# A decoder step on one core: the index-key projection moved to the two-bank group, the indexer's products spread over three query heads, the last turned chunk copied first, the samples' final sums joined

## The reference

```
q, k, v, qi, ki, wi = jnp.split(h @ w_in, ATTN_SPLITS, axis=-1)
q = rms_norm(q.reshape(B, T, N_HEADS, HEAD_DIM), g_q)
ki = rms_norm(ki, g_kidx)
...
logits = jnp.einsum('bthd,bsd->bths', qi, ki).astype(jnp.float32) * IDX_DIM ** -0.5
w = wi.astype(jnp.float32) * IDX_HEADS ** -0.5
return jnp.einsum('bth,bths->bts', w, jax.nn.relu(logits))
...
for e in range(N_EXPERTS):
    out = out + combine[:, e:e + 1].astype(t.dtype) * swiglu(t, w_gate[e], w_up[e], w_down[e])
```

## Time and profile before

| | |
|---|---|
| median of 3 runs | 1547.24 us (1545.6 to 1547.84) |
| profiled execution | 1545.37 us, span 1543.2 us |
| PE busy | 1512.4 us, 98% of the span |
| DVE busy | 1211.9 us, 79% |
| ACT busy | 979.4 us, 63% |
| POOL busy | 166.2 us, 11% |
| mean granted clock of PE | 0.994 |

### The profile page before, as it was taken

One profiled execution on the slowest core, in us unless ns is written; L12 is line 12 of the kernel. 1 busy time (PEld: TensorE's weight loads), 2 busy tenths in 40 slices (PEclk: granted clock), 3 DMA queues, 4 the chain that ended last, 5 costly groups with the idle time before them and its releaser, 6 DMA issues.

```text
span 1543.2 us, 21704 instructions
## 1 busy us (share of the span) xinstructions
PE 1512.4 (98%) x8246; PEld 1284.9 (83%) x8246; DVE 1211.9 (79%) x1127; ACT 979.4 (63%) x928; POOL 166.2 (11%) x160
## 2 busy tenths in 40 slices
PE   7899989999999999999999999999999999999998
PEld 5787768999997987888888888888888888888886
DVE  5479774666454958889889889889888888889887
ACT  3343663444344567777777777777777777777774
POOL 2455000000000014801000000000000000100000
PEclk9899999999999999999999999999999999999999
DMA  6346773343655437999999999999999999999990
GB/s 216 117 184 257 277 267 116 127 146 123 234 199 183 168 110 255 380 382 382 393 395 382 393 395 382 394 395 392 384 395 383 381 395 372 378 395 369 375 346 31
DMA packets 199014, 457.30 MB, mean 296 GB/s; under 512 B 12104, under 2 KB 15210, under 8 KB 198954
## 3 DMA queue, kind: packets, MB, share of 16 engines
q1 hardware_dynamic: 190754, 439.27, 76.9%
q0 software_dynamic: 4416, 13.15, 3.0%
q10 hardware_dynamic: 3784, 4.06, 0.8%
HBM read 444.43 MB, written 12.03 MB: 296 GB/s over the span
## 4 chain that ended last, share of the span: by engine, by line
PE 84%; DVE 2%; ACT 1%; issue 0%; DVEq 0%; ACTq 0%
PE bank L1922 18%; PE bank L2377 13%; PE bank L2379 13%; PE bank L2378 13%; PE bank L2391 7%; PE bank L2393 6%; PE bank L2392 6%; PE bank L1909 2%; PE bank L2401 2%; PE bank L2190 1%; PE bank L1917 0%; PE bank L2284 0%; PE bank L2194 0%; DVE ring_r L1348 0%; PE bank L2358 0%
## 5 line engine op out<-in xcount | busy, mean ns | idle before, releaser
L1742 DVE TENSOR_TENSOR wql<-ring,wqh 128x2048 fp32r<-128x2048 f32 x336 | 768.8, 2291 | 108.4 <-ACT wqh L933 107.9
L933 ACT ACTIVATE wqh<-ring 128x2048 fp32r<-128x2048 f32 x336 | 644.9, 1920 | 231.0 <-PE bank L2379 147.8
L2377 PE MATMUL bank<-wqh,xgh 128*128 128x512 f32 x896 | 355.3, 396 | 0.4 <-issue 0.4
L2379 PE MATMUL bank<-wqh,xgl 128*128 128x512 f32 x896 | 349.6, 390 | 0.0
L2378 PE MATMUL bank<-wql,xgh 128*128 128x512 f32 x896 | 349.1, 390 | 0.0
L2379 PEld LDWEIGHTS bank<-wqh,xgl 128*128 128x128 f32 x896 | 168.3, 188 | 36.1
L2377 PEld LDWEIGHTS bank<-wqh,xgh 128*128 128x128 f32 x896 | 168.2, 188 | 34.7 <-issue 0.8
L2378 PEld LDWEIGHTS bank<-wql,xgh 128*128 128x128 f32 x896 | 168.4, 188 | 32.9
L933 ACT ACTIVATE wd<-ring 128x1024 fp32r<-128x1024 f32 x90 | 94.8, 1058 | 129.9 <-PE bank L1922 129.8
L2391 PE MATMUL bank<-wqh,heTh 128*128 128x512 f32 x440 | 171.4, 389 | 0.0
L2393 PE MATMUL bank<-wqh,heTl 128*128 128x512 f32 x440 | 171.2, 389 | 0.0
(11 more groups left out here) (414 smaller groups left out, 2013.7 us busy)
## 6 DMA issues: line engine op xcount, KB each, us to landing
ring<-in_moe_w_gate SPq DMA_DIRECT2D x56, 2048.0 KB, 15.5
ring<-in_moe_w_up SPq DMA_DIRECT2D x56, 2048.0 KB, 15.8
ring<-in_moe_w_down SPq DMA_DIRECT2D x56, 2048.0 KB, 14.9
ring<-in_attn_w_in SPq DMA_DIRECT2D x7, 2048.0 KB, 10.4
ring<-in_ffn_w_gate SPq DMA_DIRECT2D x5, 2048.0 KB, 8.3
ring<-in_ffn_w_up SPq DMA_DIRECT2D x5, 2048.0 KB, 8.0
ring<-in_cache_k SPq DMA_DIRECT2D x16, 512.0 KB, 13.3
ring<-in_cache_v SPq DMA_DIRECT2D x16, 512.0 KB, 5.2
```

Source lines behind the costliest of these rows:

```text
L933: return nc.scalar.activation(dst, src, ACT.Copy)
L1742: return v.tensor_tensor(dst, src, head.bitcast(F32), ALU.subtract)
L2377: mm(bank, xgh[:, k, :], w_h[:, part], start=(k == 0), stop=False)
L2379: last = mm(bank, xgl[:, k, :], w_h[:, part], start=False, stop=(k == KD - 1))
```

## The change

It has four parts.

1. `ki` moves from group A to group B. Its products stay in their place. In group A the result six places ahead of `("qk", 0)` is now `wi`. ACT makes all four first weight quarters ahead of the square `kisq`; before it made two ahead of it and one behind.
2. `kio` and `("iss", 0)` move from behind head 0 to behind head 1, `("iss", 1)` to behind head 2, `isel` to behind head 3, ahead of `("is", 0)`.
3. In the last item ACT and DVE take the last turned chunk ahead of the last weight half instead of behind it.
4. At the end the two results of the samples share one bank: the first half of the columns on partitions 0 to 31, the second on 32 to 63. The matrix `pickT` gets columns of zeros on both sides of the samples' (they are there from the memset), so that each pair of products adds zeros to the other's rows. One sum of 64 rows takes the place of two of 32, and comes last. `xtok` is loaded in the same layout, the weights of the samples are copied once to partitions 32 to 63, and the last result is stored by ACT and SP, half each.

```
-    A.add("ki", "dve")
+    B.add("ki", "dve")
...
-        if n == 0:
+        if n == 1:
             A.add("kio", "act")
-            for g in range(2):
-                A.add(("iss", g), "act")
+            A.add(("iss", 0), "act")
         elif n == 2:
+            A.add(("iss", 1), "act")
+        elif n == 3:
             A.add("isel", "dve")
...
+        sp.wait_ge(sc_ok, 5)
+        sp.dma_start(o_y[1][:, 0:CH], xtok[0:NS, 2, 0:CH]).then_inc(end_stored, 16)
+        sp.wait_ge(end_stored, 16)
...
-        heads_before(2)
-        act.wait_ge(*A.full("ki"))
-        nc.scalar.activation(kisq[:], A.ap("ki")[:, 0:T], ACT.Square).then_inc(kisq_ok, 1)
-        heads_before(3)
+        heads_before(WRING)
+        act.wait_ge(*B.full("ki"))
+        nc.scalar.activation(kisq[:], B.ap("ki")[:, 0:T], ACT.Square).then_inc(kisq_ok, 1)
...
             for p in range(3, halves if last else halves + 3):
+                if last and p == halves - 1:
+                    take_heT(i, NCH - 1, heTh2)
                 head(i, HPRO + p)
...
-                    copy(pickT[:, 0:T], banks[7][:, 0:T]).then_inc(pickT_ok, 1)
+                    copy(pickT[:, 0:NP], banks[7][:, 0:NP])
+                    copy(pickT[:, NP + NS:NP + 2 * NS], banks[7][:, NP:T]).then_inc(pickT_ok, 1)
...
-            if n == 2:
+            if n == 3:
                 take_sample_scores()
...
-            m, half = k % 3, k // 3
+            m, half, r = (k % 2, k // 2, P) if k < 4 else (2, 0, 2 * NS)
             dve.wait_ge(sc_full, k + 1)
...
+                if last and p == halves - 1:
+                    heT_tails(i, NCH - 1, heTl2, heTh2)
                 tail(i, HPRO + p)
...
+        link(v.tensor_copy(comb[NS:2 * NS, 2, 1:ITEMS + 1], comb[0:NS, 2, 1:ITEMS + 1]))
         dve_body(last_item, LAST)
-        dve.wait_ge(xtok_in, 16 * 3)
-        for k in range(6):
+        dve.wait_ge(xtok_in, 16 * 4)
+        for k in range(5):
             add_back(last_item + 1, k, banks[END_BANK[k]])
...
-        project("ki", kw, 0, None, hE)
+        B.room(pe, "ki")
+        for c in range(KD):
+            last = mm(B.ap("ki")[:, 0:T], kw[:, c, 0:P], hE[:, c, :], start=(c == 0), stop=(c == KD - 1))
+        last.then_inc(b_full, 1)
...
+        def scatter_samples(half, bank):
+
+            part, left = slice(CH * half, CH * half + CH), pickT[:, NP + NS * (1 - half):NP + NS * (1 - half) + 2 * NS]
+            mm(bank[0:2 * NS, :], left, ysbh[:, part], start=(half == 0), stop=False)
+            return mm(bank[0:2 * NS, :], left, ysbl[:, part], start=False, stop=(half == 1))
```

More of the change, by code:

```diff
@@ L917, in _ @@
         pool.sem_inc(scatters, 1)
-        for m in range(3):
-            pool.dma_start(xtok[0:ROWS[m], m, :], z_rows[P * m + P:P * m + P + ROWS[m], :]).then_inc(xtok_in, 16)
+        for m in range(2):
+            pool.dma_start(xtok[:, m, :], z_rows[P * m + P:P * m + 2 * P, :]).then_inc(xtok_in, 16)
+        for half in range(2):
+            pool.dma_start(xtok[NS * half:NS * half + NS, 2, 0:CH], z_rows[3 * P:3 * P + NS, CH * half:CH * half + CH])\
+                .then_inc(xtok_in, 16)
     @block.scalar
@@ L1016, in take_indexer @@
                 copy(kitok[0:NS, 2, :], kio[0:NS, 2, 0:ID]).then_inc(a_act, 1)
[L1017 to L1020, removed]
+            if n in (1, 2):
+                g = n - 1
+                act.wait_ge(*A.full(("iss", g)))
+                nc.scalar.activation(rls[:, g, :], A.ap(("iss", g))[:, 0:WS], ACT.Relu, scale=ID ** -0.5)\
+                  .then_inc(a_act, 1)
             elif n in SCORES:
@@ L1323, in _ @@
         act_body(last_item, LAST)
-        for k in range(6):
-            m, part = k % 3, slice(CH * (k // 3), CH * (k // 3) + CH)
+        for k in range(4):
+            m, part = k % 2, slice(CH * (k // 2), CH * (k // 2) + CH)
             act.wait_ge(sc_ok, k + 1)
-            store(rows_of(o_y, m)[:, part], xtok[0:ROWS[m], m, part])
+            store(rows_of(o_y, m)[:, part], xtok[:, m, part])
+        act.wait_ge(sc_ok, 5)
+        store(o_y[1][:, CH:D], xtok[NS:2 * NS, 2, 0:CH])
         act.wait_ge(stored, 16 * N_STORED)
@@ L2022, in indexer @@
         def indexer(n):
-            if n == 0:
+            if n == 1:
                 A.room(pe, "kio")
-                pe.wait_ge(*A.freed("ki"))
+                pe.wait_ge(*B.freed("ki"))
                 for m in range(3):
@@ L2030, in indexer @@
                 pe.wait_ge(*A.freed(("qi", 3)))
[L2031 to L2043 removed]
+            if n in (1, 2):
+                g = n - 1
+                A.room(pe, ("iss", g))
+                for j in range(4):
+                    b = 4 * g + j
+                    rows = A.ap(("iss", g))[NS * j:NS * j + NS, :]
+                    q = qix[:, b, :, :].rearrange("p h t -> p (h t)")
+                    pe.wait_ge(*A.freed(("kipt", b // 2)))
+                    mm(rows[:, 0:PAST], q, kipT[:, 2 * b:2 * b + 2, :].rearrange("p a s -> p (a s)"),
+                       start=True, stop=True)
+                    last = mm(rows[:, PAST:WS], q, kiT[:, NP + TS * b:NP + TS * b + TS], start=True, stop=True)
+                last.then_inc(a_full, 1)
+            if n == 3:
                 A.room(pe, "isel")
@@ L2462, in _ @@
         pe.wait_ge(pickT_ok, 1)
-        for k in range(6):
-            pe.wait_ge(y_ok, k // 3 + 1)
-            scatter(k, banks[END_BANK[k]])
+        for half in range(2):
+            pe.wait_ge(y_ok, half + 1)
+            for m in range(2):
+                scatter(2 * half + m, banks[END_BANK[2 * half + m]])
+            last = scatter_samples(half, banks[END_BANK[4]])
+        last.then_inc(sc_full, 1)
     return ctx
-END_BANK = [0, 1, 2, 3, 6, 7]
+END_BANK = [0, 1, 2, 3, 6]
 INS = ["x_prompt", "x_sample", "cache_k", "cache_v", "cache_kidx", "page_table", "norm_mix", "norm_ffn",
```

44 lines of the change are left out of this document (15 added, 29 removed).

## The result

The changed kernel takes 1536.63 us (median of 6 runs, 1535.95 to 1537.23), the kernel before 1546.38 (6 runs, 1544.7 to 1547.84). The ratio is 0.9934, 95% interval 0.9923 to 0.9945: 9.75 us faster by the medians. The profiled execution took 1536.29 us against 1545.37, 9.08 less; 1536.3 was worked out for it ahead of the run.

A forecast was written before the change was run, and what follows sets the result against it. TensorE, busy 98% of the span, was taken as the bound. Terms 6.6 + 1.9 + 0.6 = 9.1 us off the shown median 1547.24 gave 1538.1 (1536.3 for the profiled execution), range 1536 to 1541.5.

The forecast's parts named there:

- A: Whole kernel: the forecast that all gains arrive, 9.1 us less, median 1538.1 us; chance 0.66.
- Start, 4.45 + 1.95 + 0.2 = 6.6: Ahead of and in the first query head: idle gap 4.45, lower clock 1.95; selection's bank wait 0.2; 6.6 us gained.
- D: Rival: the start's 6.6 us come to nothing, through DVE's full stretch or an unmoved load; gain 2.5, time 1544.7; chance 0.11.
- left behind head 0, they would be wanted at 52 and wait for 53.04: Indexer at the start: transposes of kiT kept behind head 0 would wait from 52 until kiT is written at 53.04.
- the spread of the indexer: Indexer's products over three heads: the selection's wait for head 0's bank goes, 0.2 us gained.
- Last turned chunk, 1.9: Last item's end: copying the turned chunk first removes PE's wait for xgl, 1.83 to 2.0, taken as 1.9 us.
- The slack of 0.5 us: Last weight half: DVE ends its subtraction at 1530.4, PE wants it at 1531.0; slack 0.5 us.
- C: Rival: PE waits for the last half tile's weights, giving back all 1.9; gain 7.2, time 1540; chance 0.09.
- Joined sums, 0.6: Samples' final adds: five DVE sums in place of six end 0.67 us sooner; 0.6 taken as gain.
- a risk: Final stores: four of 256 KB every 0.67 us need 391 GB/s against 387 moved, so they could queue a little.
- its bounds of 0.3 to 0.67: Samples' joined final adds: the gain was bounded between 0.3 and 0.67 us, with 0.6 taken.
- E: Rival: DVE's sums of scores meet POOL's tails more often, 2.1 us each; with six, time 1550.7; chance 0.04.

The follow-up runs named there:

- parts 1 and 2 alone: The kernel before with only the index-key projection in the two-bank group, early weight heads and the indexer spread over three heads: 1540.26 us, ratio 0.9969.
- part 1 alone: The kernel before with the projection's other bank and four early weight heads, indexer left behind head 0: 1539.6 us, ratio 0.9959.
- the kernel with the old order of heads: The kernel before with only the index-key projection's other bank, weight heads in their old order, indexer behind head 0: 1541.75 us, ratio 0.9974.
- the filled gap: The kernel before with 32 needless products on TensorE in the gap ahead of the first query head: 1545.88 us, ratio 1.0004.
- part 4 alone: The kernel before with only the samples' two results joined, five final sums in place of six: 1545.33 us, ratio 0.9998.
- filling the stall alone: 12 needless products in the xgl stall, added to the kernel before with the other bank, early weight heads and spread indexer: 1539.1 us, ratio 0.9957.
- the transposes: The kernel before with 36 needless full-precision transposes on TensorE in the gap ahead of the first query head: 1546.66 us, ratio 1.0008.

## Why the prediction was right, and where it was not

The forecast (A) came true: the median is 1536.63 where 1538.1 stood, within 1536.0 to 1541.5. Of the 1.5 us between them 0.9 come of the starting point (1547.24, where the kernel before has 1546.38 over six runs) and 0.65 of the gain (9.75 for 9.1). Term by term, with the profiled executions:

- **Start, 4.45 + 1.95 + 0.2 = 6.6.** Measured 6.65 at the attention's output, 6.61 counted from the index keys' sum of squares. The gap is gone, the clock stays at 1.00, the selection waits for nothing. That the 6.6 would reach the end was the larger doubt (D), and it holds: the last turn starts 6.60 earlier. In medians it is 5.3 (parts 1 and 2 alone) to 6.2 (part 1 alone), less than in this pair of profiles. Why, the runs don't settle; some profiled executions have a clock that fell elsewhere.
- **"left behind head 0, they would be wanted at 52 and wait for 53.04"** failed as a step. It took the old time of `kiT`, 53.04, and forgot what the text itself says a few lines on, that POOL's third tail no longer meets DVE's. Without that meeting one tail of 2.61 us becomes one of 0.45, and `kiT` is ready 3.64 us behind the start of the keys' sum of squares in place of 5.05, 1.4 earlier. Part 1 without part 2 shows no wait, and the kernel with the old order of heads shows one, 1.38 us at 53.26. The start works by the bank (1545.78 - 1541.75 = 4.0 us in the medians, with the old order of heads) and by the order of the weight heads (another 2.1), to which the text gave no term; the spread of the indexer, left at 0.2, doesn't show.
- **Last turned chunk, 1.9.** Measured 2.14 in the profiles (first sum 8.74 earlier, of which 6.60 were there at the turn). The term was sized by the idle time and the starts around it, 2.22 - 0.23 = 1.99; another 0.15 is that the first products behind the stall follow each other more slowly. The slack of 0.5 us ahead of the last half held (DVE is done at 1523.66, PE begins the half at 1524.20): C fell. But in the medians this part is worth 3.7, and the text has no term for it. The missing step: the stall of `xgl` stops PE just as the gap at the start did, and behind a stop the clock may fall. It didn't in the profiled execution of before, so the earlier trace rows couldn't show it. It did in four of the seven profiled kernels that have the stall (the filled gap, part 4 alone, part 1 alone with either order of heads) and in none of the seven that lack it or have it filled. By chance alone all four would lie on one given side in about 1 of 29 cases, so this is strong but not proof; there is one profile of each kernel. It costs 1.6 us when it comes, 0.9 on average by these counts (an estimate); filling the stall alone brought 1.2 in the median. 2.1 + 1.2 leaves 0.4 of the 3.7 that no run explains, which is of the size of the medians' scatter.
- **Joined sums, 0.6.** Mis-sized: 0.34. From the start of the first sum to the end of the execution the profiled kernels with six sums take 8.3 us (before: 1545.37 - 1537.10 = 8.27; six sums in the changed kernel: 1537.23 - 1528.93 = 8.30), those with five 7.9 (changed kernel: 1536.29 - 1528.36 = 7.93; part 4 alone: 1545.80 - 1537.88 = 7.92). DVE does end 0.66 earlier, and the stores are issued that much sooner, but they reach the transfer's rate, which the text had seen as a risk and had priced too low: read in windows of 0.3 us, the transfers end 5.2 us behind the first sum with six sums (the kernel before, and the changed one with six) and 4.9 with five (the changed kernel, and part 4 alone). One reserve: the 0.34 sets a time of the span against the time of the whole execution. By the span alone the end is not shorter (6.10 and 6.17 with six sums, 6.24 and 6.22 with five); what got shorter is the time outside the span, 2.1 to 2.2 us with six sums and 1.7 with five, and no row says why. Part 4 is inside its bounds of 0.3 to 0.67, at the lower one, and in the medians it is nothing.
- **E**: in the changed kernel DVE meets no more of POOL's tails than before at the sums of scores. The seven wide ones take 767 ns on average in both kernels and the seven narrow ones 348, the longest is 2.47 us against 2.48, and PE's wait is 0.5 as before.

The stores at the end of the changed kernel, windows with DMA share and GB/s in the last two columns:
```profile
1530.00:1531.00 1.00, 0.30 (x2) 0.00 (x0) 1.00 (x3) 0.00 (x0) 0.00 (x0) 1.00 0.98 377
1531.00:1532.00 1.00, 0.00 (x0) 0.00 (x0) 0.72 (x2) 0.00 (x0) 0.00 (x0) 1.00 1.02 385
1532.00:1533.00 1.00, 0.00 (x0) 0.00 (x0) 0.00 (x0) 0.00 (x0) 0.00 (x0) 1.00 0.99 348
```
And those of the kernel before, where the queue ran empty for a moment (225 GB/s) between the third store and the last ones:
```profile
1539.00:1540.00 1.00, 0.04 (x1) 0.00 (x0) 1.00 (x3) 0.00 (x0) 0.00 (x0) 1.00 0.98 377
1540.00:1541.00 1.00, 0.00 (x0) 0.00 (x0) 1.00 (x2) 0.00 (x0) 0.00 (x0) 1.00 0.65 225
```
With five sums the transfer has no such hole between 1530 and 1533.

That the sum came out at 9.08 for 9.1 in the profiles is so partly by luck, by errors that cancel: 2.14 for 1.9 and 0.34 for 0.6.

What stays open: why the kernel before scatters over almost 7 us (68 runs in the three groups) and the changed one over 1.3 (only 6 runs). The fall at the end accounts for 1.6 of it and is gone. The rest was seen in single profiles only: a start stage from 34 to 48 us with a clock of 0.76 (in the profiles of before and after) or 0.88 (in variants of both), PE's wait for the gathered rows (0.4 and 3.1 us), and a clock of 0.93 between 200 and 250 us, which came in the changed kernel's variants too. The part that no edit touches, from the attention's output to the last turn, takes 1299.4 to 1299.5 us in seven of the fourteen profiles, 1300.0 to 1301.3 in six and 1306.0 in one (the transposes), so differences of a microsecond between two single profiles, or between medians of few runs, can come from there.

## What to carry to other kernels

A stop of TensorE costs its length and, in some executions, the lower clock behind it; one profile may show the one without the other, so look at the same stretch in several profiles before pricing a stall. When a change moves one engine's work away from another's, work out the times of everything that shared the stretch anew, since the old row's time of a result already holds the meeting that is going away. And where an end is a train of stores, compare the stores' bytes over their spacing with the rate that the transfers reach: once the two are equal, fewer instructions ahead of them bring little (0.34 us here in the profiles, for 0.66 of instructions, and nothing in the medians).

## What the runs showed of the hardware that was not expected

- The granted clock fell from 1.00 to 0.50 behind a stop of 1.83 us in four of seven profiled executions (one of each kernel), and cost 1.6 us; with 12 products laid into the same stop, which left it 0.4 us, it did not fall in the one profiled.
- 36 fp32 transposes in the gap held the clock at 1.00, as 32 products did.
- The early weight heads gained 2.1 us in the medians, 1.4 of it seen in the profile, although POOL is busy 11% of the span: beside one of its 2.7 us tails, begun at 46.88, one DVE tail took 2.61 us in place of 0.45.
- Two loads of 2 MB, issued 2.85 us earlier, reached PE only 1.5 us earlier (14.78 us from issue to use in place of 13.43), while ten loads of cached keys were issued behind them in place of nine.
